# Two weight sums formed on the Vector engine instead of by adding DMAs, in a fused two-layer block on one Trainium2 core

## The chip, the cores and the metric

The program runs on 1 core of a Trainium2 chip. A core has a matrix engine (TensorE: PE in the rows, PEld for its weight loads), a Vector engine (DVE), a Scalar engine (ACT), GpSimd (POOL), a Sync engine (SP) whose queue issues most DMAs, and 16 DMA engines that move data between the chip's memory and the on-chip memory. The metric is the device time of one execution in microseconds (us), lower is better. The kernel before takes 2440.25 us (median of 3 runs, 2436.58 to 2447.19).

## The reference

The reference runs one sequence of 256 rows, 2048 wide, through a mixer layer, a pooling layer and an attention layer. All of it is computed in float32. What the change touches is the feed-forward part that follows the mixer and the pooling, twice in all:

```python
for i in range(2):
    ...                                    # mixer (i = 0) or pooling (i = 1), residual into x
    h = rmsnorm(x, g[2])                   # 256 x 2048
    f = jnp.square(jax.nn.relu(h @ mlp_w1[i])) @ mlp_w2[i]   # 2048 -> 8192 -> 2048
    x = x + rmsnorm(f, g[3])
```

## The kernel before

**Split products.** Every float32 weight tile (128 partitions x 2048 numbers, 1 MB) is split on the chip into a high part (ACT, line 495, two halves of 1024) and a low part (DVE, line 614, raw minus high, again two halves). A product is three matrix multiplications: high x high, high x low, low x high (line 351). A tile feeds 12 of them when 128 rows are multiplied and 24 when 256 are. The high and low parts live in a ring of 3 operand buffers, so the split of a tile waits until the tile three places earlier has been used, half by half. Raw tiles land in a ring of 3 raw buffers (`raw`, loads of line 1015 on SP's queue); a raw buffer is free when its low part is made.

**Up-projection with seven products.** The 8192 columns of `mlp_w1` are worked off in 8 blocks of 1024 columns. The first block is a plain product. For each of the 7 other blocks (`both_ways`, e = 1 to 7), which I call a round, rows, depth and columns are each halved and the 2x2 block product is formed with seven instead of eight products, Winograd's way. With B11, B12 (left half of the depth, two column halves of 512) and B21, B22 (right half), the seven steps use these weights, each of two tiles (j = 0, 1):

- up 1: B11. up 2: B21. up 3: B22.
- up 5: B11+B12, called T1. up 6: B11+B12+B22. up 4: B11+B12+B22+B21.
- up 7: B12+B22, called T3.

B11, T1 and the two longer sums are one chain: two fixed buffers in `R_f` (`chain`) are loaded with B11 by SP (`chain_load`, line 1019), and after each split of them `link` lets a DMA from POOL's queue add the next block to them in place (`chain_add`, line 1007). T3 is made in the raw ring: SP loads B12 and a POOL DMA adds B22 to it (`add_tile`, line 1002). POOL's engine only issues these DMAs.

**Order of a round.** Down-projection tiles of the block before (`down`, 24 multiplications, two banks that are freed by DVE's `R_m` sums of line 599) stand between the up steps, which take turns in two other banks. The tiles of a round in order, with up steps of two tiles and down steps of one: up 1, down 0, up 2, down 1, up 5, down 2, up 3, down 3, up 6, down 4, up 7, down 5, up 4, down 6, four pairs of transposes (line 354), down 7. The outputs of the seven products are put together from staging tiles `EV` by DVE (`combine`, line 599) and squared by ACT (lines 551 and 553: relu, square). What each engine does is written in one fixed order: `take` and `release` emit the splits of tiles some places ahead, and each engine works its own list strictly in order. So a split that stands behind a `combine` in DVE's list waits for it, and a relu that stands before a split in ACT's list holds it up.

**Around it.** `x_columns` normalizes and transposes the residual `X` (2 MB, resident all the time) ahead of a projection; for a projection with no filler work between, it splits the first weight tile in four quarters. At the start of the program tiles 0 to 2 of `w_z` land at once and tile 3 waits for a raw buffer.

## Time and profile before

| | before |
|---|---|
| median of 3 runs | 2440.25 us |
| the profiled execution | 2433.57 us |
| its span | 2431.7 us |
| PE busy | 95% |
| DVE busy | 67% |
| ACT busy | 54% |
| POOL busy | 5% |
| granted TensorE clock, mean | 0.978 |
| DMA | 563.60 MB, mean 232 GB/s |

PE's share is high, but the end of a multiplication is modelled in the records, so "busy" isn't the same as full pace. The profiled execution is 6.7 us below the median of the runs; steps are worked out against the former and then set beside the latter. The rounds of the two feed-forward parts lie between about 454 and 1112 us and between about 1283 and 1940 us of the span.

### The profile page before, as it was taken

The page shows a single profiled execution, that of the slowest core. Times are in us where ns is not written, and L with a number is a line of the kernel's source. Part 1 is how long each engine was busy: PE and PEld are TensorE (multiplying, and loading weights), DVE is VectorE, ACT ScalarE, POOL GpSimd, SP SyncE. Part 2 cuts the span into 40 slices and gives each one's busy share as a digit, 9 for nine tenths or more (in the row PEclk, how much of TensorE's full clock was granted, in tenths as well). Part 3 has the DMA queues.
Part 4 walks back from the last instruction along what each step waited for, and adds up shares of the span by engine and source line. Part 5 has one row for each costly group of instructions (what it writes and reads, how often), then busy time and mean ns, then how long its engine had stood idle before and what let it go on. Part 6 is the DMA issues. An engine that isn't in the chain of part 4 may idle for free.

```text
span 2431.7 us, 26613 instructions
## 1 busy us (share of the span) xinstructions
PE 2312.5 (95%) x10609; PEld 1898.8 (78%) x10609; DVE 1623.3 (67%) x2015; ACT 1321.8 (54%) x1769; POOL 127.4 (5%) x160
## 2 busy tenths in 40 slices
PE   9999999999889899899999989899899899999998
PEld 6778888778778677777887777787777788888887
DVE  5665856866667667667877667667666676556764
ACT  6355445655646556555666646556556555444453
POOL 0000000001001001010001000000000001000000
PEclk9999999999999999999999999999999999999999
DMA  8444545889899898896658898998998845653343
GB/s 332 157 173 173 184 164 190 239 279 275 277 278 254 262 294 254 257 283 228 225 208 233 272 289 252 262 293 264 254 283 269 251 141 201 244 214 129 140 172 121
DMA packets 80299, 563.60 MB, mean 232 GB/s; under 512 B 9033, under 2 KB 9364, under 8 KB 14319
## 3 DMA queue, kind: packets, MB, share of 16 engines
q1 hardware_dynamic: 61568, 429.58, 47.1%
q0 software_dynamic: 18464, 132.20, 26.2%
q8 instruction: 84, 1.38, 0.2%
q14 instruction: 39, 0.32, 0.0%
q10 hardware_dynamic: 144, 0.12, 0.0%
HBM read 559.77 MB, written 2.10 MB: 231 GB/s over the span
## 4 chain that ended last, share of the span: by engine, by line
PE 59%; DMA 23%; DVE 9%; ACT 4%; issue 2%; POOL 1%; ACTq 0%; POOLq 0%; DVEq 0%
PE P L351 56%; DMA R_f<-in_w_u 15%; DVE low L614 7%; DMA raw<-in_w_d 5%; ACT hi L495 3%; DMA raw<-in_w_u 3%; PE P L354 3%; DVE EV L599 1%; DVE R_m L599 1%; ACT EV L551 1%; POOL raw L1002 0%; ACT R_h L490 0%; POOL R_f L1007 0%; DVE R_f_r L599 0%; DVE X L602 0%
## 5 line engine op out<-in xcount | busy, mean ns | idle before, releaser
L614 DVE TENSOR_TENSOR low<-raw,hi 128x1024 fp32r<-128x1024 f32 (+3 forms) x752 | 879.6, 1203 | 535.8 <-ACT hi L495 532.7
L495 ACT ACTIVATE hi<-raw 128x1024 fp32r<-128x1024 f32 (+3 forms) x752 | 758.3, 1039 | 551.2 <-PE P L351 315.4
L351 PE MATMUL P<-hi,R_h 128*128 128x512 f32 (+2 forms) x2944 | 954.9, 395 | 8.4 <-DVE low L614 8.1
L351 PE MATMUL P<-hi,R_f_r 128*128 128x512 f32 x2480 | 822.4, 405 | 96.7 <-DVE R_m L599 52.7
L351 PEld LDWEIGHTS P<-hi,R_h 128*128 128x128 f32 x2944 | 554.4, 189 | 131.4 <-DVE low L614 12.7
L351 PEld LDWEIGHTS P<-hi,R_f_r 128*128 128x128 f32 x2480 | 483.7, 195 | 211.9 <-DVE low L614 109.1
L351 PE MATMUL P<-low,R_h 128*128 128x512 f32 (+2 forms) x1472 | 572.4, 389 | 0.0
L351 PE MATMUL P<-low,R_f_r 128*128 128x512 f32 x1240 | 497.6, 401 | 0.0
L614 DVE TENSOR_TENSOR low<-R_f,hi 128x1024 fp32r<-128x1024 f32 x224 | 264.5, 1221 | 94.1 <-ACT hi L495 92.4
L351 PEld LDWEIGHTS P<-low,R_h 128*128 128x128 f32 x1472 | 278.0, 189 | 56.3 <-issue 4.3
L495 ACT ACTIVATE hi<-R_f 128x1024 fp32r<-128x1024 f32 x224 | 227.7, 1052 | 100.6 <-DMA R_f<-in_w_u 66.4
L351 PEld LDWEIGHTS P<-low,R_f_r 128*128 128x128 f32 x1240 | 242.6, 196 | 49.4
L351 PE MATMUL P<-hi,R_g_r 128*128 128x512 f32 x448 | 142.6, 389 | 0.0
L551 ACT ACTIVATE EV<-EV,st 128x512 f32<-128x512 f32 x56 | 40.5, 723 | 167.5 <-DVE EV L599 167.5
L1007 POOL DMA_DIRECT2D R_f<-in_w_u x84 | 78.0, 1039 | 871.7 <-DVE low L614 871.7
L351 PEld LDWEIGHTS P<-hi,R_g_r 128*128 128x128 f32 x448 | 84.1, 188 | 17.4
L351 PE MATMUL P<-low,R_g_r 128*128 128x512 f32 x224 | 87.2, 389 | 0.0
L599 DVE TENSOR_TENSOR R_m<-P,R_m 128x512 f32<-128x512 f32 x112 | 71.9, 683 | 0.0
L351 PE MATMUL P<-hi,R_s_r 128*128 128x512 f32 x224 | 71.3, 389 | 0.0
L354 PE MATMUL P<-ident,EV 128*128 128x128 f32 (+1 forms) x476 | 66.4, 272 | 0.0
L354 PEld LDWEIGHTS P<-ident,EV 128*128 128x128 f32 (+1 forms) x476 | 56.7, 139 | 9.1
L599 DVE TENSOR_TENSOR R_f_r<-P,R_f_r 128x512 fp32r<-128x512 f32 x66 | 42.6, 684 | 26.4 <-ACT R_f_r L490 26.4
(216 smaller groups left out, 1260.4 us busy)
## 6 DMA issues: line engine op xcount, KB each, us to landing
raw<-in_w_d SPq DMA_DIRECT2D x128, 1024.0 KB, 8.4
raw<-in_w_u SPq DMA_DIRECT2D x100, 1024.0 KB, 5.2
R_f<-in_w_u POOLq DMA_DIRECT2D x84, 1024.0 KB, 11.9
raw<-in_w_z SPq DMA_DIRECT2D x46, 1024.0 KB, 4.9
raw<-in_w_i SPq DMA_DIRECT2D x36, 1024.0 KB, 4.8
R_f<-in_w_u SPq DMA_DIRECT2D x28, 1024.0 KB, 7.9
raw<-in_w_u POOLq DMA_DIRECT2D x28, 1024.0 KB, 10.4
raw<-in_w_mo SPq DMA_DIRECT2D x16, 1024.0 KB, 4.9
```

What stands on the lines that cost most here:

```text
L351: return self.e.matmul(o, l, r, start=start, stop=stop, skip_group_check=True)
L354: return self.e.transpose(o, i, self.m.ident[0:i.shape[0], 0:i.shape[0]])
L495: self.e.activation(hi, raw, ACT.Copy).then_inc(*self.inc("high_made", ("high", k, d)))
L551: self.e.activation(o, p, ACT.Relu, scale=r).then_inc(*self.inc("act_done", evacuated))
L599: self.e.tensor_tensor(o, a, b, op).then_inc(*self.inc("dve_done", *done))
L614: self.e.tensor_tensor(low, raw, hi.bitcast(f32), ALU.subtract).then_inc(*self.inc("low_made", *lows))
L1007: self.e.dma_start(o, i, accum_op=ALU.add).then_inc(*self.landed(f"added{j}", done))
```

## The change

1. T1 and T3 are formed by DVE. Two more fixed buffers, `chain[2]` and `chain[3]`, hold B12; they are the memory of `X`. Once B11 has been split, DVE adds B12 onto it (`first_sum`, giving T1 in `chain[j]`). B22 is loaded once, as a plain raw tile of kind "kept"; after its split DVE adds it onto B12 (`third_sum`, giving T3 in `chain[j + 2]`), and only then its raw buffer is free. `add_tile` is gone, and `link` keeps two adding DMAs per j, for B22 and B21.
2. `X` is stored to a scratch tensor in the chip's memory after the first up group (`keep_x`), and is loaded again after the last round (`back`), before the residual needs it.
3. Products 1 and 2 accumulate in one bank, and products 5 and 3 in the other. Copies of products 1 and 5 are taken in between, and the multiplications of the second product wait for that copy (`onto`). DVE's `combine` of products 1+2 and of 5+3 goes; the bank of 5+3 is read by the second `combine` after up 6 and is free after it.
4. Tile 3 of `w_z` gets its own landing place in `R_f` and isn't behind the raw ring.
5. In `x_columns` the last sums of row half 0 (`out_of`, `squares_of`) stand ahead of the first two quarter splits.

```diff
@@ -149,6 +149,7 @@
 NO = 3
 AHEAD = 2
 CHAIN = (0, 4, 6, 2)
+FIRST = 3
...
-        self.chain = [R_f[:, 4096:6144], R_f[:, 6144:8192]]
+        self.chain = [R_f[:, 4096:6144], R_f[:, 6144:8192], self.X[:, 0, :], self.X[:, 1, :]]
+        self.first_raw = R_f[:, 0:2048]
...
+    def tile_sum(self, o, i, ready, done):
+        self.wait_ge(ready)
+        self.tt(o, o, i, ALU.add, done)
...
-    def load_tile(self, k, o, i, l, free):
-        self.wait_ge(free)
-        self.e.dma_start(o, i).then_inc(*self.landed(f"ring{l % NL}", ("loaded", k)))
+    def load_tile(self, k, o, i, ring, free):
+        self.wait_ge(free)
+        self.e.dma_start(o, i).then_inc(*self.landed(ring, ("loaded", k)))
...
-                raw = m.raw[l % NL][0:parts, 0:c]
-                E.load_tile(k, raw, a[name][i], l, freed.get(l - NL))
-                if kind == "sum":
-                    E.add_tile(k, raw, a[name][more], l)
+                E.load_tile(k, m.raw[l % NL][0:parts, 0:c], a[name][i], f"ring{l % NL}", freed.get(l - NL))
+            elif k == FIRST:
+                E.load_tile(k, m.first_raw, a[name][i], "ring3", None)
...
         if kind == "chain":
-            raw, ready = m.chain[more[3]], ("chained", *more)
+            raw, ready = m.chain[more[3] + 2 * (more[2] == 4)], ("chained", *more)
+        elif k == FIRST:
+            raw, ready = m.first_raw, ("loaded", k)
         else:
-            raw, ready = m.raw[l % NL], ("tile sum", k) if kind == "sum" else ("loaded", k, 2 * d // n) if k < 2 else ("loaded", k)
+            raw, ready = m.raw[l % NL], ("loaded", k, 2 * d // n) if k < 2 else ("loaded", k)
...
                 link(*more, ("low", k, 3))
-            else:
+            elif kind == "load" and l is not None:
                 freed[l] = ("low", k, 3)
                 load_ahead()
...
     def link(mlp_, e, s, j, free):
-        s, e = (s + 1) % 4, e + (s == 3)
-        i, done = 8 * e + CHAIN[s] + j, ("chained", mlp_, e, s, j)
-        if e == 8:
-            chain_last[j] = free
-        elif s == 0:
-            E.chain_load(j, m.chain[j], a[f"w_u{mlp_}"][i], free, done)
+        w = a[f"w_u{mlp_}"]
+        if s == 0:
+            return
+        if s in (1, 2):
+            E.chain_add(j, m.chain[j], w[8 * e + CHAIN[s + 1] + j], free, ("chained", mlp_, e, s + 1, j))
+        elif e == 7:
+            chain_last[j + 2 * (s == 4)] = free
+        elif s == 3:
+            E.chain_load(j, m.chain[j], w[8 * e + 8 + j], free, ("chained", mlp_, e + 1, 0, j))
         else:
-            E.chain_add(j, m.chain[j], a[f"w_u{mlp_}"][i], free, done)
-
-    chain_last = [None, None]
+            E.chain_load(j + 2, m.chain[j + 2], w[8 * e + 12 + j], free, ("linked", mlp_, e + 1, j))
+
+    chain_last = [None] * 4
...
         if filler is None:
             quarter = quarters()
+            out_of(0)
+            squares_of(0)
             quarter(0)
             quarter(1)
-            out_of(0)
-            squares_of(0)
             start(0, lambda: (quarter(2), quarter(3)))
...
+
+        def keep_x():
+            kept = side_load("kept", a["x_kept"], m.X.rearrange("p t n -> p (t n)"), list(x_m))
+            for j in range(2):
+                E.chain_load(j + 2, m.chain[j + 2], a[up_w][12 + j], [kept, list(h_m), list(r_m)], ("linked", l, 1, j))
...
                 if g == 0:
+                    keep_x()
...
-        def half_product(b, xh, xl, ready, tiles, end, soon):
+        def half_product(b, xh, xl, ready, tiles, end, soon, onto, aside):
 
             for n, tile in enumerate(tiles):
                 j, wh, wl = take(up_w, *tile)
+                if n == 0:
+                    aside()
                 wh, wl = v3(wh, 4), v3(wl, 4)
                 for k in range(4):
-                    x = ready[4 * n + k] if isinstance(ready, list) else ready
+                    x = [ready[4 * n + k] if isinstance(ready, list) else ready, onto]
                     whose = ([("product", j, 1)] if k == 3 else []) + ([("used", j, k // 2)] if k % 2 else [])
                     E.product(P[b][:, :], xh[:, 4 * n + k, :], xl[:, 4 * n + k, :], wh[:, k, :], wl[:, k, :], j, k,
-                              n == k == 0, n == 1 and k == 3, x, bank_free[b], *whose)
+                              onto is None and n == k == 0, n == 1 and k == 3, x, bank_free[b], *whose)
                 if n == 1 and soon:
                     end(b, ("product", j, 1))
                 release(j, ("product", j, 1))
...
+            def copied(n, b, done):
+                k, name = ev(hold=True), mark("product copied")
+                E.copy_out(EV[k][:, :], P[b][:, :], done, ev_free[k], name)
+                ks[n], ms[n] = k, name
+
             def first(b, done):
-                k, name = ev(hold=True), mark("product 1")
-                E.copy_out(EV[k][:, :], P[b][:, :], done, ev_free[k], name)
-                bank_free[b] = [name]
-                ks[1], ms[1] = k, name
+                copied(1, b, done)
 
             def second(b, done):
-                k = ev(hold=True)
-                c11 = combine(k, P[b][:, :], EV[ks[1]][:, :], ALU.add, [done, ms[1]], ev_free[k])
-                bank_free[b] = [c11]
-                ks[11] = k
-                ms[11] = relu_square(k, EV[k][:, :], 0, c11, None)[1]
-                ms[1] = c11
+                ks[11] = k = ev(hold=True)
+                evacuated, ms[11] = relu_square(k, P[b][:, :], 0, done, ev_free[k])
+                bank_free[b] = [evacuated]
 
             def fifth(b, done):
-                k, name = ev(hold=True), mark("product 5")
-                E.copy_out(EV[k][:, :], P[b][:, :], done, ev_free[k], name)
-                bank_free[b] = [name]
-                ks[5], ms[5] = k, name
+                copied(5, b, done)
 
             def third(b, done):
-                k = ev(hold=True)
-                ks[12] = k
-                ms[12] = combine(k, P[b][:, :], EV[ks[5]][:, :], ALU.add, [done, ms[5]], ev_free[k])
-                bank_free[b] = [ms[12]]
+                box["w"] = b, done
 
...
             def sixth(b, done):
                 ms[1] = combine(ks[1], P[b][:, :], EV[ks[1]][:, :], ALU.add, [done, ms[1]])
                 bank_free[b] = [ms[1]]
-                c12 = combine(ks[12], EV[ks[12]][:, :], EV[ks[1]][:, :], ALU.subtract, [ms[12], ms[1]])
-                ms[12] = relu_square(ks[12], EV[ks[12]][:, :], 0, c12, None)[1]
-                ms[1] = c12
+                wb, w_done = box["w"]
+                ks[12] = k = ev(hold=True)
+                c12 = combine(k, P[wb][:, :], EV[ks[1]][:, :], ALU.subtract, [w_done, ms[1]], ev_free[k])
+                bank_free[wb] = [c12]
+                ms[12] = relu_square(k, EV[k][:, :], 0, c12, None)[1]
...
             def seventh(b, done):
                 ms[1] = combine(ks[1], P[b][:, :], EV[ks[1]][:, :], ALU.add, [done, ms[1]])
                 bank_free[b] = [ms[1]]
                 c22 = combine(ks[5], EV[ks[5]][:, :], EV[ks[1]][:, :], ALU.subtract, [ms[5], ms[1]])
                 ms[5] = relu_square(ks[5], EV[ks[5]][:, :], 1, c22, None)[1]
-                ms[1] = c22
...
+            kept_at = at_["take"] + 9
+
+            def first_sum(j):
+                E.tile_sum(m.chain[j], m.chain[j + 2], [("chained", l, e, 0, j), ("linked", l, e, j)], ("chained", l, e, 1, j))
+
+            def third_sum(j):
+                k = kept_at + j
+                landed = None if listing else plan[k][6]
+                done = ("chained", l, e, 4, j)
+                E.tile_sum(m.chain[j + 2], m.raw[(landed or 0) % NL][:, :], [("linked", l, e, j), ("loaded", k)], done)
+                if not listing:
+                    freed[landed] = done
+                    load_ahead()
...
             up(1, 0, HH[:, HLEFT, TOP], HL[:, HLEFT, TOP], h_left, linked(0), first)
-            down(0)
-            up(2, 1, HH[:, HRIGHT, TOP], HL[:, HRIGHT, TOP], h_right, plain(b21), second)
+            down(0, lambda: first_sum(0))
+            up(2, 0, HH[:, HRIGHT, TOP], HL[:, HRIGHT, TOP], h_right, plain(b21), second, onto=ms[1], aside=lambda: first_sum(1))
             if e == 1:
                 flush()
             down(1)
-            up(5, 0, SH[1], SL[1], s_m[1], linked(1), fifth)
-            down(2)
-            up(3, 1, SH[4], SL[4], s_m[4], plain(b22), third)
+            up(5, 1, SH[1], SL[1], s_m[1], linked(1), fifth)
+            down(2, lambda: third_sum(0))
+            up(3, 1, SH[4], SL[4], s_m[4], plain(b22, "kept"), third, onto=ms[5])
             down(3)
-            up(6, 0, SH[2], SL[2], s_m[2], linked(2), sixth)
+            up(6, 0, SH[2], SL[2], s_m[2], linked(2), sixth, aside=lambda: third_sum(1))
             down(4)
-            up(7, 1, SH[3], SL[3], s_m[3], added, seventh)
+            up(7, 1, SH[3], SL[3], s_m[3], linked(4), seventh)
             down(5)
             up(4, 0, HH[:, HRIGHT, BOTTOM], HL[:, HRIGHT, BOTTOM], h_right, linked(3), fourth, True)
...
         row_m.append(side_load("gain", m.gain_row, a["rows"][row].partition_broadcast(128), chain_last[0]))
+        back = [side_load(f"back{t}", m.X[:, t, :], a["x_kept"][:, 2048 * t:2048 * t + 2048], chain_last[2 + t]) for t in range(2)]
```

How the lists move. First DVE's list before, in a round, from the splits of the tiles of up 3 and down 3 to those of up 4 (`low<-raw` is the split of a raw tile, `low<-R_f` that of a chain tile, `R_m` the sum of a down bank, `EV` a combine; x6 stands for six in a row, two per tile):

```order
L614 TENSOR_TENSOR low<-raw,hi 128x1024 [waits s_high_made] x6
L614 TENSOR_TENSOR low<-R_f,hi 128x1024 [waits s_high_made] x4
L599 TENSOR_TENSOR EV<-P,EV 128x512 [waits s_act_done,s_product_done]
L614 TENSOR_TENSOR low<-raw,hi 128x1024 [waits s_high_made] x2
L599 TENSOR_TENSOR R_m<-P,R_m 128x512 [waits s_product_done]
L599 TENSOR_TENSOR R_m<-P,R_m 128x512
L614 TENSOR_TENSOR low<-raw,hi 128x1024 [waits s_high_made] x4
L599 TENSOR_TENSOR EV<-P,EV 128x512 [waits s_dve_done,s_product_done]
L599 TENSOR_TENSOR EV<-EV 128x512 [waits s_dve_done]
L614 TENSOR_TENSOR low<-raw,hi 128x1024 [waits s_high_made] x2
L614 TENSOR_TENSOR low<-R_f,hi 128x1024 [waits s_high_made] x4
L599 TENSOR_TENSOR EV<-P,EV 128x512 [waits s_dve_done,s_product_done]
```

The same place of DVE's list in the changed kernel:

```order
L616 TENSOR_TENSOR low<-raw,hi 128x1024 [waits s_high_made] x4
L601 TENSOR_TENSOR X<-X,raw 128x2048 [waits s_ring1]
L616 TENSOR_TENSOR low<-raw,hi 128x1024 [waits s_high_made] x2
L616 TENSOR_TENSOR low<-R_f,hi 128x1024 [waits s_high_made] x4
L616 TENSOR_TENSOR low<-raw,hi 128x1024 [waits s_high_made] x2
L601 TENSOR_TENSOR R_m<-P,R_m 128x512 [waits s_product_done]
L601 TENSOR_TENSOR R_m<-P,R_m 128x512
L601 TENSOR_TENSOR X<-X,raw 128x2048 [waits s_ring2]
L616 TENSOR_TENSOR low<-X,hi 128x1024 [waits s_high_made] x4
L601 TENSOR_TENSOR EV<-P,EV 128x512 [waits s_act_done,s_product_done]
L601 TENSOR_TENSOR EV<-P,EV 128x512 [waits s_dve_done]
L616 TENSOR_TENSOR low<-raw,hi 128x1024 [waits s_high_made] x2
```

The combine after up 3 is gone, a tile sum stands behind the splits of up 3's tiles and another one behind the sums of down 3, and up 7's tiles are split from `X` behind it. Both combines after up 6 now read a bank, and they stand behind up 7's splits.

SP's list in one round before (`in_w_d` are down tiles, `in_w_u` up tiles, `R_f` the chain):

```order
L1015 DMA raw<-in_w_u 128x2048 [waits s_low_made] x2
L1015 DMA raw<-in_w_d 128x2048 [waits s_low_made] x2
L1015 DMA raw<-in_w_u 128x2048 [waits s_low_made] x2
L1015 DMA raw<-in_w_d 128x2048 [waits s_low_made] x2
L1015 DMA raw<-in_w_u 128x2048 [waits s_low_made] x2
L1015 DMA raw<-in_w_d 128x2048 [waits s_low_made] x4
L1019 DMA R_f<-in_w_u 128x2048 [waits s_low_made] x2
```

And in the changed kernel, from the same chain loads on:

```order
L1016 DMA raw<-in_w_u 128x2048 [waits s_low_made] x2
L1016 DMA raw<-in_w_d 128x2048 [waits s_low_made] x2
L1016 DMA raw<-in_w_u 128x2048 [waits s_low_made] x2
L1016 DMA raw<-in_w_d 128x2048 [waits s_low_made]
L1016 DMA raw<-in_w_d 128x2048 [waits s_dve_done] x2
L1016 DMA raw<-in_w_d 128x2048 [waits s_low_made] x2
L1020 DMA X<-in_w_u 128x2048 [waits s_low_made] x2
L1016 DMA raw<-in_w_d 128x2048 [waits s_low_made]
L1020 DMA R_f<-in_w_u 128x2048 [waits s_low_made] x2
```

The two later loads of up tiles per round (B12 for T3) are gone, two loads into `X` are new, and two down tiles (those of down 4 and down 5) now wait for DVE's tile sums instead of a split. The load of down 6 stands behind them.

## Rows read from the trace of the kernel before

**Rows 1.** the page, part 1, whole span: busy time, share of the span, instructions.

```profile
PE 2312.5 (95%) x10609; PEld 1898.8 (78%) x10609; DVE 1623.3 (67%) x2015; ACT 1321.8 (54%) x1769; POOL 127.4 (5%) x160
```

**Rows 2.** windows, four rounds: length, busy us (instructions) by engine, PEclk, DMA, GB/s.

```profile
737.80:833.20 95.40, 87.14 (x378) 70.83 (x377) 63.41 (x63) 52.79 (x59) 6.98 (x8) 0.96 0.91 265
...
sum 378.70, PE 349.72 PEld 285.19 DVE 254.16 ACT 213.24 POOL 28.18; mean PE 87.43 PEld 71.30 DVE 63.54 ACT 53.31 POOL 7.05
```

**Rows 3.** the chain of waits, 735 to 930 us: start us, us, what.

```profile
737.81 19.10 PE P L351 x84
...
776.87 5.20 DMA raw<-in_w_u
...
783.42 26.69 DMA R_f<-in_w_u
...
814.23 0.70 DVE EV L599
...
817.32 2.36 DVE low L614 x2
819.68 0.61 DVE R_m L599
...
820.42 8.27 PE P L351 x24
828.70 0.87 PE P L354 x8
```

**Rows 4.** timeline of PE, 797 to 836 us: start, us, what [idle before, releaser].

```profile
803.81 0.50 PE L351 MATMUL P<-hi,R_f_r 128*128 128x512 f32 x1 [3.14 <-DVE low L614]
...
820.42 0.76 PE L351 MATMUL P<-hi,R_f_r 128*128 128x512 f32 x1 [4.89 <-DVE R_m L599]
```

**Rows 5.** timeline of PE, 533 to 545 us.

```profile
536.36 0.47 PE L351 MATMUL P<-hi,R_f_r 128*128 128x512 f32 x1 [2.25 <-ACT R_m L490]
...
536.90 0.62 PE L351 MATMUL P<-hi,R_f_r 128*128 128x512 f32 x2
```

**Rows 6.** DMA, 642.2 to 1020.8 us: queues; issues, KB, median us to landing.

```profile
q0 software_dynamic: 4769, 34.74, 45.9%
q1 hardware_dynamic: 9216, 67.11, 45.6%
...
raw<-in_w_d SPq DMA_DIRECT2D x32, 1024.0 KB, 8.8
```

**Rows 7.** source line 599, 0 to 460 us: duration ns min/median/max, starts.

```profile
L599 DVE TENSOR_TENSOR R_f<-R_f x2: 2291/2292/2294, 114.8 to 117.1; 128x2048 f32<-128x2048 f32 x2
```

**Rows 8.** timeline of ACT, 800 to 803 us.

```profile
800.17 0.72 ACT L551 ACTIVATE EV<-EV,st 128x512 f32<-128x512 f32 x1 [2.88 <-DVE EV L599]
800.93 0.63 ACT L553 ACTIVATE EV<-EV 128x512 f32<-128x512 f32 x1
801.46 1.99 ACT L495 ACTIVATE hi<-raw 128x1024 fp32r<-128x1024 f32 x2
```

**Rows 9.** waits of PE, whole span: us in total, times, longest.

```profile
PE P L351 <- DVE R_m L599: 52.7, 12, 4.9
PE P L351 <- DVE low L614: 47.4, 28, 3.1
```

**Rows 10.** DMA issues, whole span: KB each, median us to landing.

```profile
R_s<-in_memt POOLq DMA_DIRECT2D x1, 2048.0 KB, 12.8
```

**Rows 11.** timeline of PE, 0 to 30 us.

```profile
26.00 0.47 PE L351 MATMUL P<-hi,R_h 128*128 128x512 f32 x1 [1.89 <-DVE low L614]
```

**Rows 12.** timeline of all engines, 1980 to 1992 us.

```profile
1984.19 1.05 DVE L614 TENSOR_TENSOR low<-raw,hi 128x396 fp32r<-128x396 f32 x2 [3.25 <-ACT hi L495]
...
1985.16 0.68 DVE L599 TENSOR_TENSOR R_m<-P,R_m 128x512 f32<-128x512 f32 x1
...
1988.67 1.42 DVE L602 SCALAR_TENSOR_TENSOR X<-R_m,st,X 128x512 f32<-128x512 f32 x2
1989.48 1.78 PE L354 MATMUL P<-ident,X 128*128 128x128 f32 x8 [3.24 <-DVE X L602]
```

More of the change, by code:

```diff
@@ L343 @@
         product = norm_mean = norm_part = norm_whole = norm_root = relu_square = residual = rope = rope_keys = scale = scaled_parts = scores = side_load = side_taps = sine = sine_of = \
[L344 removed]
+        split = square_sum = store = tile_sum = chain_load = chain_add = combine = operand_sum = times_row = times_row_apart = pads = group_sums = tail_keys = tail_rows = turn = v_times_k = values = warm = y_back = idle
 class Pe(Engine):
@@ L997, in side_load @@
         self.e.dma_start(o, i).then_inc(*self.landed(sem, done))
-    def add_tile(self, k, o, i, l):
-        self.wait_ge(("loaded", k))
-        self.e.dma_start(o, i, accum_op=ALU.add).then_inc(*self.landed(f"sum{l % NL}", ("tile sum", k)))
     def chain_add(self, j, o, i, free, done):
@@ L1137, in take @@
             l = o = None
-            if kind != "chain":
+            if kind != "chain" and j != FIRST:
                 l = numbers["landing"]
@@ L2017, in mlp @@
         flush()
-        return residual(sums, gm, gain_apart if late else gain_of, out_of, squares_of, apart=late)
+        return residual(sums, gm, gain_apart if late else gain_of, out_of, squares_of, back, late)
     memory = {}
```

17 lines of the change are left out of this document (8 added, 9 removed).

## The prediction

> **What bounds the kernel now.** I read the page first: PE is busy for 95% of the span, DVE for 67% [rows 1]. That says where to look for losses: not in an engine that is full, but in the places where PE stands. PE's own waits give two large groups, 52.7 us behind DVE's sums of the down banks and 47.4 us behind low parts [rows 9]. Nearly all of both lie in the 14 rounds.
>
> Next, the windows over four whole rounds: 378.7 us, so 94.7 us a round, with the DMA engines 0.91 busy and DVE at 63.5 us a round [rows 2]. What would a round take if PE never stood? 84 multiplications at full pace took 19.10 us, 0.2274 us each [rows 3]. A round has 7 up steps and 8 down steps of 24, so 360 multiplications: 81.9 us. Two groups of transposes at 0.87 us [rows 3] bring it to 83.6 us. So about 11.1 us a round are lost, 155 us in 14 rounds.
>
> The chain of waits says to what. In the round from 737.8 us it leaves PE, goes to the landing of a raw up tile (5.20 us), then to one adding DMA that took 26.69 us, then through a combine (0.70), a split (2.36) and a bank's sum (0.61) back to PE [rows 3]. PE's timeline shows the two holes: 3.14 us before down 5 and 4.89 us before down 6 [rows 4]. After the second the first multiplication takes 0.76 us instead of 0.50 [rows 4], and the 24 of down 6 take 8.27 us [rows 3] instead of 24 x 0.2274 = 5.46. So a round loses about 8.0 us by standing and 2.8 us by half pace.
>
> Why is the adding DMA that slow? In 378.6 us the adding queue q0 moved 34.74 MB, which is 33 tiles, and held the 16 engines for 45.9%: 5.27 us a tile. The plain queue q1 moved 64 tiles in 45.6%: 2.70 us a tile [rows 6]. A round has 8 adds and 16 plain loads, 42.2 + 43.2 = 85.4 us of 94.7. The DMA engines are nearly full, and everything that is late is late behind them.
>
> **The change part by part.**
>
> DMA: a round now has 4 adds and 16 plain loads (the chain's B11, X's B12, B21, B22, eight down tiles): 21.1 + 43.2 = 64.3 us. In a round of 85 us that is 0.75. Before, the two adds for T3 and the chain's last two are issued close together, and the landing of 26.69 us is one of these; the adds that remain are two pairs, three steps apart.
>
> DVE: four tile sums of 128x2048 are added. A DVE sum of that shape took 2.29 us [rows 7], so +9.2 us. Two combines go, -1.4 us. DVE comes to 63.5 + 7.8 = 71.3 us a round. ACT's work stays: its copies are the same, and the relu of products 1+2 reads the bank. PE still has 360 multiplications, and the copies of products 1 and 5 that it now waits for lie beside down 0 and down 2, 5.46 us each.
>
> Where does DVE's list end last? I set up 1 at 0 and count PE in steps of 5.46: down 3 ends at 43.7, up 6 at 49.1, down 4 at 54.6. The first tile sum stands before down 1's split; from the round before's list DVE gets there at about 10.5, and up 5's tiles are ready at 20.0 and 22.4, wanted at 21.8 and 24.5. The tile sum for j=0 of T3 ends at 33.6; down 4's load waits for it and has until 42 to land, 8.4 us.
> The tight place begins at 43.7, when down 3 has freed its operand. High half 1.05, low half 1.2, two bank sums of 0.65: 47.2. Tile sum: 49.5. Splits of up 7's two tiles: 54.2. Two combines of 0.7: 55.6. Up 7 wants at 54.6 the bank that the second combine frees, so PE stands 1.0 us. Then ACT's relu and square, 1.3 us [rows 8], high half 1.0, low 2.4: down 5's tile is ready from 59.1, wanted at 61.1. Its load was free to start at 49.5 (it waits for the tile sum) and is wanted at 56.9, so 7.4 us; down tiles landed in 8.8 us (median) in the crowded stretch [rows 6]. At 0.75 instead of 0.91 I take it as just in time. Splits of up 4: 65.0, combines 66.4, ACT 67.7, split of down 6 to 71.2, bank sum 71.8, wanted at 72.0. So by this timetable 1.0 us is lost, at the start of up 7. Several margins are under 1 us, so I take 2.0 us: a round of 85.6 us.
>
> Does half pace come back with a hole that short? After a hole of 2.25 us the next multiplications ran at full pace, two in 0.62 us [rows 5]; the hole of 4.89 us [rows 4] was followed by half pace. I take none. The Trainium skill speaks against me: TensorE: Matmul & The Clock Gate, section "A second HAM failure mode: psum-queue depth-cycling", has small idle times between groups of matmuls, repeated, that let the clock go back and forth. Rows 5 do not agree with it for one such hole; no row shows holes of 1 us in each round.
>
> The rounds: 94.7 - 85.6 = 9.1 us, x 14 = 127 us.
>
> X's store and reload: 2 MB out, beside the second up group. The nearest row is a 2 MB load on the same queue, 12.8 us [rows 10]. SP's two loads into X wait for it with the loads of later tiles behind them. Counted from the start of the second up group, the store lands at 12.8, the two X tiles by about 22 (8.8 for the first), the next raw tile, up 2's second, at 25. It is wanted after four tiles of that group, up 1, down 0 and half of up 2, 35.5, less its split, so at 33. Cost 0. If the store took twice as long, the first round would stand 5 us, twice in the program: bounds 0 and +10 us. The reload starts with the last splits of up 7 and has down 5 to down 7 and eight more down tiles, over 50 us: 0.
>
> Tile 3's own place: PE stood 1.89 us for it at 26.00 us [rows 11]. Its load now doesn't wait for a split, but the columns of the input are still being prepared on ACT and DVE: -1.5 us, bounds 0 and -3.
>
> The order at the tail: row half 0's last bank sum of DVE ran at 1985.16, behind a quarter's splits of 1984.19 that wait for PE, and X followed at 1988.67 with PE standing 3.24 us [rows 12]. The bank had been finished one group of multiplications earlier. Ahead of the splits, the sum and the root can be done before PE is through: -3 us here, -1 us ahead of the first feed-forward part, bounds 0 and -5.
>
> Sum against the profiled execution: 2433.6 - 127 - 1.5 - 4 = 2301. The median of the runs is 6.7 us above the profiled execution, so 2308; for the margins under 1 us, which can only fail on one side, I add a fifth of a microsecond a round and say 2311.
>
> **The rivals.**
>
> *DVE takes over (A).* DVE has 71.3 us of work in 85.6, and after each combine it waits for ACT's relu, square and high half, 2.4 us, three times a round: 78.5 us. If a raw tile is late by 2 us at down 4 or down 5, or a split slips, the loss before up 7 and down 6 grows to what it is now less the clock's part, 5 to 6 us a round. For it: the chain already runs through combines and splits [rows 3]. Against: today the same list starts late only because it waits for DMAs. Round 89.1: 5.6 x 14 = 78, time 2440 - 78 - 5 = 2357.
>
> *Half pace stays (B).* The holes shrink but the clock still drops once a round: 2.8 x 14 = 39 us more, 2350. It is the mechanism of the skill's page above, priced by rows 3.
>
> *The raw ring chokes (C), the other side.* Two of three raw buffers are held by B22 until DVE's tile sums, and SP's list stops there with the loads of down 4, 5, 6 and 7, and behind them X's and the chain's. If landing from that point took 20 us or more, as the add of 26.69 us did [rows 3], down 5 would be 12.6 us late each round, more than the 11.1 that can be won: 14 x 1.5 = 21 us slower and up, 2460. It decides from a landing of about 18.5 us. Against: plain loads took 8.8 us (median) even at 0.91 [rows 6].
>
> *The transfers were hidden anyway (D).* If down 5 and 6 were held by the combines' place in the list alone, nothing changes: 2435. Against: DVE sat waiting for landed tiles in just these holes.
>
> **How the numbers follow.** Forecast 0.68, A 0.17, B 0.08, C 0.03, D 0.04. Range: PE's floor gives 2440 - 155 + a little for pauses that can't go, so 2290 at the low end; the high end takes in B and A, 2362. A measurement of this kernel can tell about 0.5%, 12 us, from no change. Faster by more: 0.93 (forecast, A, B). Within: 0.04 (D). Slower: 0.03 (C).
>
> **What would show it.** Rounds of 85 to 86 us in the windows, DMA share near 0.75, DVE near 71 us a round. PE's holes of 3.1 and 4.9 us gone, a new one of about 1 us at the first multiplication of up 7, PEclk at 1.0 in the rounds. The 128x2048 sums at 2.29 us. No wait of SP's list over 15 us behind `kept`. No hole at 26.0 us and a shorter one before the attention projection. I am wrong if down 4 or down 5 waits for its landing in most rounds, or if the hole before down 6 is still over 3 us.

## The result and the profile after

| | before | after |
|---|---|---|
| median (runs) | 2438.41 us (4) | 2308.36 us (4) |
| lowest to highest | 2434.93 to 2447.19 | 2307.69 to 2310.81 |
| ratio [95%] | | 0.946 [0.944, 0.949] |
| the profiled execution | 2433.57 us | 2310.81 us |
| its span | 2431.7 us | 2309.0 us |
| granted TensorE clock, mean | 0.978 | 0.996 |

The change makes the kernel 5.4% faster. The forecast was 2311 us. The page's part 1 of the kernel after (busy us, share of the span, instructions) answers to [rows 1]:

```profile
PE 2272.0 (98%) x10609; PEld 1873.5 (81%) x10609; DVE 1717.7 (74%) x2043; ACT 1318.4 (57%) x1769; POOL 81.1 (4%) x110
```

The windows of the kernel after over eleven whole rounds, each from one up 7 to the next (one of the eleven rows, and their sum; columns as in [rows 2]):

```profile
771.50:856.50 85.00, 84.01 (x376) 69.01 (x376) 70.56 (x70) 54.16 (x67) 4.25 (x5) 1.00 0.74 242
...
sum 935.80, PE 922.66 PEld 760.09 DVE 768.29 ACT 581.00 POOL 39.48; mean PE 83.88 PEld 69.10 DVE 69.84 ACT 52.82 POOL 3.59
```

935.8 / 11 = 85.07 us a round against 94.7 [rows 2]. The granted clock is 1.00 in all eleven, and the DMA engines are busy for 0.74 to 0.78 of a round instead of 0.91. The holes of 3.14 and 4.89 us [rows 4] are gone. PE's three largest waits in the whole span (total us, times, longest), beside [rows 9]:

```profile
PE P L353 <- DVE EV L601: 10.7, 12, 0.9
PE P L353 <- DVE low L616: 9.2, 5, 2.9
PE P L353 <- DVE R_m L601: 3.5, 5, 1.1
```

52.7 us behind the bank sums became 3.5, and 47.4 behind low parts became 9.2. New is the first row: one hole of 0.9 us in 12 of the 14 rounds, behind a `combine`. PE's timeline of the kernel after shows where (start, us, what, [idle before, releaser]); R_h starts up 7:

```profile
482.61 0.80 PE L353 MATMUL P<-hi,R_s_r 128*128 128x512 f32 x1 [2.91 <-DVE low L616]
483.63 1.06 PE L353 MATMUL P<-hi,R_s_r 128*128 128x512 f32 x2
...
489.48 0.61 PE L353 MATMUL P<-hi,R_f_r 128*128 128x512 f32 x2
...
856.53 0.47 PE L353 MATMUL P<-hi,R_h 128*128 128x512 f32 x1 [0.89 <-DVE EV L601]
...
874.19 0.47 PE L353 MATMUL P<-hi,R_f_r 128*128 128x512 f32 x1 [1.06 <-DVE R_m L601]
...
1866.16 1.32 PE L356 MATMUL P<-ident,X 128*128 128x128 f32 x8 [1.59 <-DVE X L604]
```

The first rows are the first round of a part: a hole of 2.91 us, then two multiplications in 1.06 us instead of 0.61 for about 6 us; the granted clock from 483.61 to 489.61 us was 0.57, near the lower of its two levels, 1.2 GHz. The last row is the tail: 1.59 us instead of 3.24 [rows 12].

The path into the 0.9 us hole is DVE's. Its timeline of the kernel after, from the place where down 3 frees its operand (844.78 us; ACT's high half starts there, and the second of the first two low halves waits for it):

```profile
844.57 2.56 DVE L616 TENSOR_TENSOR low<-raw,hi 128x1024 fp32r<-128x1024 f32 x2
847.04 1.28 DVE L601 TENSOR_TENSOR R_m<-P,R_m 128x512 f32<-128x512 f32 x2
848.24 2.28 DVE L601 TENSOR_TENSOR X<-X,raw 128x2048 f32<-128x2048 f32 x1
850.44 4.62 DVE L616 TENSOR_TENSOR low<-X,hi 128x1024 fp32r<-128x1024 f32 x4
854.98 1.41 DVE L601 TENSOR_TENSOR EV<-P,EV 128x512 f32<-128x512 f32 x2
```

Low parts, bank sums, T3's second tile sum, up 7's splits, two combines: 844.78 to 856.39 us, and PE starts up 7 at 856.53. Nothing in it waits for a transfer. The DMA view of the kernel after, 620 to 970 us (packets, MB, share; issues with KB and median us to landing):

```profile
q1 hardware_dynamic: 9444, 68.72, 49.8%
q0 software_dynamic: 2448, 17.83, 25.9%
...
raw<-in_w_d SPq DMA_DIRECT2D x32, 1024.0 KB, 8.8
...
R_f<-in_w_u POOLq DMA_DIRECT2D x16, 1024.0 KB, 10.2
...
R_s<-in_mem POOLq DMA_DIRECT2D x1, 1024.0 KB, 5.6
```

68.72 MB are 65.5 tiles and 0.498 x 350 us is 174.3: 2.66 us a plain tile. The 17 tiles of q0 held the 16 engines for 90.7 us, 5.33 us each. One of them, `R_s<-in_mem`, is a plain load; at 2.66 us it leaves 88.0 us for 16 adds, 5.50 each. The 33 tiles of [rows 6] hold the same plain load, which the prediction counted as an add: 5.35 instead of 5.27 for the 32 adds. The prices are nearly those of before; there are only half as many adds.

### The profile page after: what moved, and what is told of

Read it like the earlier page. It is cut to its first block, busy times and chain, and to the rows that moved or that the text cites. A ratio compares the mean times of both kernels' runs of the same rounds, so it can differ in the third digit from the quotient of the medians.

```text
span 2309.0 us, 26586 instructions
## 1 busy us (share of the span) xinstructions
PE 2272.0 (98%) x10609; PEld 1873.5 (81%) x10609; DVE 1717.7 (74%) x2043; ACT 1318.4 (57%) x1769; POOL 81.1 (4%) x110
## 4 chain that ended last, share of the span: by engine, by line
PE 82%; DVE 10%; DMA 3%; ACT 2%; issue 1%; POOL 0%; ACTq 0%; POOLq 0%; DVEq 0%
PE P L353 80%; DVE low L616 6%; DMA raw<-in_w_d 3%; PE P L356 3%; ACT hi L497 1%; DVE R_m L601 1%; DVE X L601 1%; DVE EV L601 1%; DVE R_f L601 0%; DVE R_f_r L601 0%; DVE X L604 0%; ACT EV L553 0%; DVE R_h L604 0%; DVE R_g_r L601 0%; DVE st L604 0%
## 5 line engine op out<-in xcount | busy, mean ns | idle before, releaser
L616 DVE TENSOR_TENSOR low<-raw,hi 128x1024 fp32r<-128x1024 f32 (+3 forms) x694 | 810.2, 1200 | 409.1 <-ACT hi L497 406.5
L497 ACT ACTIVATE hi<-raw 128x1024 fp32r<-128x1024 f32 (+3 forms) x694 | 701.7, 1040 | 473.9 <-PE P L353 332.4
L353 PE MATMUL P<-hi,R_f_r 128*128 128x512 f32 x2480 | 792.8, 392 | 5.3 <-DVE R_m L601 3.5
L353 PEld LDWEIGHTS P<-hi,R_f_r 128*128 128x128 f32 x2480 | 465.8, 188 | 107.4 <-DVE low L616 7.7
L353 PE MATMUL P<-low,R_f_r 128*128 128x512 f32 x1240 | 482.9, 389 | 0.0
L353 PEld LDWEIGHTS P<-low,R_f_r 128*128 128x128 f32 x1240 | 233.1, 188 | 46.5
L553 ACT ACTIVATE EV<-EV,st 128x512 f32<-128x512 f32 x42 | 30.4, 724 | 152.8 <-DVE EV L601 152.8
L1008 POOL DMA_DIRECT2D R_f<-in_w_u x56 | 48.7, 869 | 1027.2 <-DVE low L616 1027.2
L497 ACT ACTIVATE hi<-X 128x1024 fp32r<-128x1024 f32 x56 | 57.6, 1057 | 32.0 <-DVE X L601 24.9
L616 DVE TENSOR_TENSOR low<-X,hi 128x1024 fp32r<-128x1024 f32 x56 | 64.7, 1218 | 0.0
## 6 DMA issues: line engine op xcount, KB each, us to landing
X<-in_w_u SPq DMA_DIRECT2D x28, 1024.0 KB, 12.8
```

The costliest lines, as they stand in the source:

```text
L353: return self.e.matmul(o, l, r, start=start, stop=stop, skip_group_check=True)
L497: self.e.activation(hi, raw, ACT.Copy).then_inc(*self.inc("high_made", ("high", k, d)))
L553: self.e.activation(o, p, ACT.Relu, scale=r).then_inc(*self.inc("act_done", evacuated))
L616: self.e.tensor_tensor(low, raw, hi.bitcast(f32), ALU.subtract).then_inc(*self.inc("low_made", *lows))
L1008: self.e.dma_start(o, i, accum_op=ALU.add).then_inc(*self.landed(f"added{j}", done))
```

## The experiments

Each was run beside the kernel before on the same chip. Its median was 2434.4 us beside e1 to e4, 2438.3 beside e5 to e8, 2440.1 beside e9 to e11 and 2438.3 beside e12, so ratios are what compare, and a difference of two ratios is uncertain by 0.003 to 0.004. "b" is a diff against the kernel before, "a" against the kernel after.

| run | median us | ratio [95%] |
|---|---|---|
| kernel after | 2308.4 | 0.946 [0.944, 0.949] |
| e1: before, adds as plain loads | 2290.2 | 0.941 [0.939, 0.943] |
| e2: before, product pairs | 2425.2 | 0.996 [0.995, 0.998] |
| e3: after, no product pairs | 2312.7 | 0.950 [0.948, 0.952] |
| e4: T3 by DVE, T1 by DMA | 2293.1 | 0.942 [0.940, 0.944] |
| e5: T1 by DVE, T3 by DMA | 2473.1 | 1.014 [1.011, 1.018] |
| e6: after, 4 more adds a round | 2396.3 | 0.983 [0.980, 0.987] |
| e7: after, banks swapped | 2307.2 | 0.947 [0.944, 0.949] |
| e8: after, edges undone | 2310.8 | 0.948 [0.945, 0.951] |
| e9: e4 + e7 | 2292.2 | 0.939 [0.938, 0.941] |
| e10: e4, no product pairs | 2300.8 | 0.943 [0.941, 0.944] |
| e11: e9 + rows early | 2290.1 | 0.938 [0.937, 0.940] |
| e12: e11, banks as in e4, sum ahead | 2287.2 | 0.938 [0.936, 0.941] |

### Is it the adding?

**e1_plain_adds** (b): the same transfers at the same places, issued as plain copies. The sums themselves are left out: only the last block lands.

```diff
-        self.e.dma_start(o, i, accum_op=ALU.add).then_inc(*self.landed(f"sum{l % NL}", ("tile sum", k)))
+        self.e.dma_start(o, i).then_inc(*self.landed(f"sum{l % NL}", ("tile sum", k)))
...
-        self.e.dma_start(o, i, accum_op=ALU.add).then_inc(*self.landed(f"added{j}", done))
+        self.e.dma_start(o, i).then_inc(*self.landed(f"added{j}", done))
```

> The kernel before, with its 8 adding DMAs a round issued as plain loads from the same queue at the same places (the weight sums are left out of the result: only the last block lands). Lists of all engines are those of before. Theory T (the DMA engines are nearly full with the adds, so tiles land late, and that makes the holes): 24 plain loads x 2.70 us = 64.8 us a round instead of 85.4, DMA share about 0.7, holes before down 5 and down 6 go, rounds 85 to 86 us, time about 2310 to 2320. Rival R (the combines' places in the lists make the holes, whatever the DMA engines do): rounds stay at 94 us, time 2430 to 2440.

Measured: 2290.2 us. Windows and DMA of e1, 620 to 970 us:

```profile
620.00:970.00 350.00, 350.00 (x1585) 290.61 (x1585) 268.28 (x272) 229.50 (x262) 19.24 (x36) 1.00 0.80 301
```

```profile
q1 hardware_dynamic: 9423, 68.55, 52.6%
q0 software_dynamic: 5040, 36.70, 27.5%
```

PE is busy for all 350 us, which is why the time lies 20 us below the expected one: nothing is left of the waits in these rounds. q0's 35 tiles cost 0.275 x 350 / 35 = 2.75 us each instead of 5.27, and no tile is late. So the loss of the kernel before is the price of adding, not the number of bytes and not the order of the lists: e1 moves more GB/s (301) than the kernel before (265 in [rows 2]) and never stands.

**e6_traffic** (a): the reverse. Four adding DMAs a round of 1 MB, from memory to a scratch tensor that nobody reads.

```diff
+    def idle_add(self, i, free):
+        self.wait_ge(free)
+        n = self.counts.value.get("idle", 0) // 16
+        self.e.dma_start(self.a["x_idle"][n], i, accum_op=ALU.add, max_dma_last_dim=8192).then_inc(*self.landed("idle"))
```

> The changed kernel with 4 more adding DMAs of 1 MB a round on the adding queue, from w_u into scratch in the chip's memory that nobody reads, two where the add for T1 was issued before and two just before T3's tile sums. No engine but the queue waits for them. The destination is memory, not the on-chip tile, so their time may differ from 5.27 us. Theory T: DMA share back over 0.9, chain adds and down tiles late, holes of several us a round, 2350 to 2440. Theory T2: the chain's last adds are late behind the extra ones but T3 isn't: 2310 to 2350. Rival R: 2308.

Measured: 2396.3 us. Waits of PE in the whole span and windows, 620 to 970 us, of e6:

```profile
PE P L353 <- DVE low L616: 66.9, 31, 3.5
```

```profile
620.00:970.00 350.00, 329.95 (x1465) 269.45 (x1464) 274.62 (x260) 206.89 (x243) 28.77 (x34) 1.00 0.93 278
```

As many adds as before bring back two thirds of what had been won (88 of 130 us), but not the waits of the kernel before. The chain of waits of e6, before down 5:

```profile
693.85 2.21 DVE X L601
696.08 11.78 DMA raw<-in_w_d
```

Its split follows, and PE starts down 5 at 710.25, 2.50 us late. What is late is a plain down tile: its load starts when DVE's tile sum has freed the raw buffer, and down tiles took 11.8 us (median) instead of 8.8. That is rival C's link at a lower price. The chain's adds landed in 10.5 us (median), as in the kernel after. So e6 shows that adding traffic in the background costs the rounds time; it does not show the link through which the kernel before lost it. That is left to e4 and e5.

### Which sum pays?

**e4_t3_by_dve** (a): T1 by adding DMAs again, T3 stays with DVE.

```diff
-        if s == 0:
-            return
-        if s in (1, 2):
+        if s in (0, 1, 2):
...
-            down(0, lambda: first_sum(0))
+            down(0)
```

> The changed kernel with T1 formed by an adding DMA of B12 again and T3 still by DVE: 6 adds and 16 plain loads a round, 31.6 + 43.2 = 74.8 us of DMA. Theory T in its simple form (share of the DMA engines alone counts): share 0.87, partway back, 2330 to 2370. Theory T2 (only the burst of T3's two adds beside the chain's last two is late): no loss, and DVE has 4.6 us a round less: 2300 to 2310. Rival R: as the changed kernel, 2308.

**e5_t1_by_dve** (a): the other half. `first_sum` stays, T3 is made in the raw ring by `add_tile` again.

```diff
+            if kind == "sum":
+                E.add_tile(k, m.raw[l % NL][:, :], a[name][more], l)
...
-            down(2, lambda: third_sum(0))
+            down(2)
...
-            up(7, 1, SH[3], SL[3], s_m[3], linked(4), seventh)
+            up(7, 1, SH[3], SL[3], s_m[3], [(8 * e + 4 + j, "sum", b22[j]) for j in range(2)], seventh)
```

> The mirror of the last one: T1 formed by DVE, T3 by a load into the raw ring and an adding DMA as before. 6 adds and 18 plain loads a round, 31.6 + 48.6 = 80.2 us of DMA. Theory T2 (the add into the raw ring for T3, issued close to the chain's last two adds and waited for by up 7's splits, is what is late; T1's add isn't): holes before down 5 and down 6 stay, 2400 to 2440. Theory T (share of the DMA engines alone): 0.9, so about as far back as T3 by DVE alone was with 0.89: about 2295 to 2330.

Measured: e4 2293.1 us, e5 2473.1 us. One half of the change is worth more than the whole, the other half alone is slower than the kernel before. Windows (620 to 970 us) and waits of PE, first of e4, then of e5:

```profile
620.00:970.00 350.00, 346.42 (x1560) 286.06 (x1559) 273.95 (x269) 221.73 (x259) 22.98 (x27) 1.00 0.89 274
```

```profile
PE P L353 <- DVE EV L601: 10.6, 12, 0.9
PE P L353 <- DVE low L616: 4.3, 2, 3.2
```

```profile
620.00:970.00 350.00, 315.10 (x1380) 257.65 (x1379) 244.44 (x239) 197.05 (x232) 18.77 (x22) 0.95 0.82 259
```

```profile
PE P L353 <- DVE EV L601: 112.9, 14, 10.5
PE P L353 <- DVE R_m L601: 17.8, 12, 2.4
```

The DMA share doesn't order them: e4 is at 0.89 and has only the 0.9 us hole, e5 is at 0.82 and stands 5.9 to 10.5 us before each up 7. Part of e5's low share is that its rounds are longer, but the work of the DMA engines per round doesn't order the kernels either: about 85 us in the kernel before, 80 in e5, 75 in e4.

What PE waits for before up 7 in e5 is T3's own second add. POOL issues it at 696.89 us, after waiting for the load of B12 under it. The timelines of ACT and DVE of e5, with up 7 starting at 714.06:

```profile
709.13 2.00 ACT L497 ACTIVATE hi<-raw 128x1024 fp32r<-128x1024 f32 x2 [4.91 <-DMA raw<-in_w_u]
710.22 2.36 DVE L616 TENSOR_TENSOR low<-raw,hi 128x1024 fp32r<-128x1024 f32 x2 [4.56 <-ACT hi L497]
712.50 1.41 DVE L601 TENSOR_TENSOR EV<-P,EV 128x512 f32<-128x512 f32 x2
```

The add has landed after 12 us, its split follows, and behind it in the list the two combines that free up 7's bank. The chain of waits of e5 names the transfer behind the next hole, before down 6:

```profile
697.97 25.98 DMA R_f<-in_w_u
...
725.06 2.36 DVE low L616 x2
727.42 0.61 DVE EV L601
```

It is the same link as in [rows 3] (26.69 us there): the chain's last add, issued behind the two adds of T3. The kernel before has both: T3's second add ahead of the hole before down 5, the chain's last ahead of the one before down 6. With T3's adds gone no chain add took over 14.1 us (e4, 500 to 1100 us; 27.1 in the kernel before), though T1's two are there. So what costs is T3's two adds, not four adds more in a round; T1's are issued right after up 1's splits and had room. How much of it is the bundle of four, and how much the order of POOL's list, is not separated: the chain's last two adds stand there behind the wait for B12's landing too, and e4 takes away both. Nor was it taken further why e5 is over 40 us slower than e2, the kernel before with the pairs alone, and above its expected range; in its chain of waits the two plain loads ahead of the adds took 11.5 and 6.8 us instead of the 8.7 and 5.2 of the kernel before.

And why does e4 beat the kernel after, by 11 us in the ratios and 15 in the medians? Both have the same 0.9 us hole. Set the starts of up 7 in the two profiled executions against each other. From the marker ahead of the rounds to up 7 of the second round the kernel after takes 195.1 us and e4 190.1; from the last up 7 of the first part to up 7 of the second part's second round 340.2 and 334.2. So the opening of each part costs 5 to 6 us. Another 0.85 us on average goes in each of the five rounds between in the first part, in holes before down 6 (behind `R_m`) that e4 doesn't have: 15.2 us together. The chain of waits of the kernel after, first round, shows DVE's list from end to end:

```profile
464.14 2.35 DVE low L616 x2
466.50 1.20 DVE R_f_r L601 x2
467.69 0.18 DVE R_f L601
...
472.16 1.14 DVE R_g_r L601
473.30 2.20 DVE R_f L601
...
481.43 1.15 DVE low L616
```

In this round DVE also makes the sums of the operands (`R_f_r`, `R_g_r`), and the T1 tile sums (`R_f`, 467.69 and 473.30) come on top. The list ends 2.91 us late, and half pace follows here; the hole of 2.90 us at the same place of the second part (1251.54) is followed by full pace. e4 has no hole of that kind there; one of 1.04 us comes at 515.16 us, at full pace.

### The product pairs

**e2_pairs_only** (b) and **e3_no_pairs** (a): item 3 of the change alone, and the change without it. Both are the same edit, one way and the other:

```diff
-                E.copy_out(EV[k][:, :], P[b][:, :], done, ev_free[k], name)
-                bank_free[b] = [name]
...
-                c11 = combine(k, P[b][:, :], EV[ks[1]][:, :], ALU.add, [done, ms[1]], ev_free[k])
+                evacuated, ms[11] = relu_square(k, P[b][:, :], 0, done, ev_free[k])
```

> The kernel before plus only the accumulation of products 1+2 and 5+3 in one bank each; the sums stay adding DMAs. Theory T: late landings stay, 2425 to 2445 (two combines of 0.7 us a round less on DVE, none of them on the late chain; at most 1 us a round, 14 us). Rival R: the two combines gone from DVE's list take most of the holes away, 2330 to 2370.

> The changed kernel with the products combined by DVE as before, sums still by DVE. Theory T: DVE gets 1.4 us a round more, 71.2; the bank of up 7 is free earlier, so the hole of 0.9 us before it goes; the splits behind the combines come later by up to 1.4 us. 2305 to 2320. Rival R: the holes come back, 2380 or more.

Measured: e2 2425.2, e3 2312.7 us. The pairs are worth 9 us on the kernel before. On top of the sums they are worth 9 us by the ratios (0.950 against 0.946) and 4 by the medians, which come from different chips; the intervals of the ratios touch. PE's waits in e2 tell of a side effect:

```profile
PE P L351 <- DVE EV L599: 81.4, 14, 8.0
PE P L351 <- DVE R_m L599: 19.7, 12, 2.9
```

The bank of 5+3 is free only after up 6's second combine, and in e2 that stands in DVE's list behind splits of a T3 tile that lands late: PE stands before up 7 (7.47 us at 517.09) instead of before down 5, and for less before down 6 (19.7 us in all against 52.7). The landing was the cause in both places.

**e10_t3_no_pairs** (a) is e4 with e3's edit.

> T3 by DVE, T1 by an adding DMA, products combined by DVE as before (no accumulation in one bank). The hole of 0.89 us before up 7 goes, as the bank isn't held; DVE has 1.4 us a round more. If DVE isn't the bound here: 12 x 0.89 = 11 us faster than T3 by DVE alone, 2282. If the 2 combines delay the splits behind them: 2293 or more.

Measured: 2300.8 us, beside 2292.2 of e9 on the same chip, which differs from it by the pairs and by two swapped banks (worth nothing in e7, below). That is 8 us, as much as the ratios give in the two cases above, and the second case of what was expected. PE's timelines show where most of it lies: e10 has a hole of 2.71 and one of 2.74 us in the opening rounds of the two parts (485.17 and 1246.94), followed by a granted clock of 0.72 and 0.76 for 6 us, and e9 has none there.

### The hole that is left

**e7_banks** (a): up 7 uses the other bank, which is free long before, and up 4 the one of 5+3.

```diff
-            up(7, 1, SH[3], SL[3], s_m[3], linked(4), seventh)
+            up(7, 0, SH[3], SL[3], s_m[3], linked(4), seventh)
...
-            up(4, 0, HH[:, HRIGHT, BOTTOM], HL[:, HRIGHT, BOTTOM], h_right, linked(3), fourth, True)
+            up(4, 1, HH[:, HRIGHT, BOTTOM], HL[:, HRIGHT, BOTTOM], h_right, linked(3), fourth, True)
```

> The changed kernel with the banks of up 7 and up 4 swapped, so that up 7 takes the bank that the first combine after up 6 frees, not the one of the second. If the hole of 0.89 us before up 7 is the wait for that bank, it shrinks by one combine, 0.69 us, to 0.2: at most 12 x 0.69 = 8 us faster than the changed kernel, 2300; as far as the hole before down 6 then grows instead (DVE's list ends no earlier), less, down to 0.

Measured: 2307.2 us, the same. The hole before up 7 shrinks from 0.89 to 0.16 us, and the holes before down 6 grow from 3.5 us in 5 rounds to 6.7 us in 12, up to 1.3 us each (0.84 at 700.28 us in e7). DVE's list from down 3 to down 6 is as long as before, and PE meets its end at the next place. **e9_t3_banks**, the same on e4, likewise:

> T3 by DVE, T1 by an adding DMA, and the banks of up 7 and up 4 swapped. With the sum of T1 off DVE its list has 4.6 us a round to spare, so the shortened hole before up 7 should not come back before down 6: 12 x 0.72 = 8.6 us faster than T3 by DVE alone (2293), 2284. If DVE's list still ends last, 2292.

Measured: 2292.2 us; ratio 0.939 against 0.942 of e4, intervals that meet.

**e12_sum_ahead** (a; e11 with the banks as in e4) takes work out of that stretch: T3's second tile sum is done inside down 3.

```diff
-            down(3)
-            up(6, 0, SH[2], SL[2], s_m[2], linked(2), sixth, aside=lambda: third_sum(1))
+            down(3, lambda: third_sum(1))
+            up(6, 0, SH[2], SL[2], s_m[2], linked(2), sixth)
```

> T3 by DVE, T1 by an adding DMA, X's rows early, banks of up 7 and up 4 as in the changed kernel, and DVE's second tile sum moved from behind the sums of down 3 to ahead of the split of down 4 (in the middle of down 3). If the chain of a round is the one of the timetable (down 3's operand free, split, bank sums, tile sum, two splits, two combines, ACT, split, bank sum, down 6), 2.3 us of it go ahead of its start: the hole of 0.89 us before up 7 goes and none comes before down 6. 2280. If the holes have another cause, 2290.

Measured: 2287.2 us, the lowest median of all, but with the ratio of e11 (0.938, 6.2% below the kernel before): the step can't be told from zero, and the 2280 expected was missed. The hole before up 7 is gone in most rounds; PE's timeline of e12 shows the one before down 6 still there:

```profile
675.19 0.47 PE L353 MATMUL P<-hi,R_h 128*128 128x512 f32 x1 [0.66 <-DVE EV L601]
...
692.83 0.47 PE L353 MATMUL P<-hi,R_f_r 128*128 128x512 f32 x1 [1.07 <-DVE R_m L601]
```

I had read the two holes as one shortage of DVE's list. The second doesn't follow from the first. It may come from the path combine, relu, square, high half, low part behind up 7's end, which a shorter list ahead of up 7 leaves as it is; that wasn't tested.

### The edges

**e8_no_edges** (a): items 4 and 5 undone.

```diff
-FIRST = 3
+FIRST = -1
...
-            out_of(0)
-            squares_of(0)
             quarter(0)
             quarter(1)
+            out_of(0)
+            squares_of(0)
```

> The changed kernel with its two edits outside the rounds undone (tile 3 of w_z again in the raw ring; the quarter splits again ahead of the last sums). By the forecast these two gave 1.5 + 4 = 5.5 us: 2314. By the two traces the start gave 0.5 and the tail 1.7: 2310.5.

Measured: 2310.8 us, 2.5 us above the kernel after (4 by the ratios), with intervals that overlap: it can't be told from zero. In the trace the tail's hole of 3.2 us is back.

**e11_rows_early** (a): e9, and the rows 2 and 3 of X are loaded ahead of the small tables at the start.

```diff
     first_rows(1)
+    first_rows(2)
+    first_rows(3)
```

> As e9, with the last two parts of X's rows loaded right behind the first two at the start, so that they don't stand behind three loads of w_z that wait for splits. The hole of 3.2 us near 39 us waits for their squares; it should go, with the half pace behind it: 3 to 5 us faster than e9, 2280.

Measured: 2290.1 against 2292.2 us of e9 on the same chip; again within the intervals. In the trace the hole near 39 us is gone, as expected (3.43 us in e9, none over 0.5 in e11).

## Why the prediction was right

**The rounds: 85.6 forecast, 85.07 measured.** Most steps behind it held. The DMA share came out at 0.765 (0.75 forecast), DVE at 69.8 us a round (71.3), the 128x2048 sums at 2.28 us (2.29 of [rows 7]), the timetable from the end of down 3's operand to the last combine at 11.6 us (11.9), the hole before up 7 at 0.89 us (1.0; with the margins I took 2.0). The timetable worked because it wrote DVE's whole list down with durations of the trace, and found the wait that would be last once the transfers were early.

**The sum over the rounds: 127 forecast, 121 measured.** From a marker ahead of the rounds (405.40 us before, 404.89 after) to the one ahead of the attention part (1989.48 and 1866.16) 122.8 us were won; 1.65 of them are the shorter hole at the second marker, so 121.2 are the rounds'. The starts of up 7 in PE's timelines divide them (us; part 1 and part 2 are the two feed-forward parts):

| | marker | part 1, first up 7 | last up 7 | part 2, first up 7 | last up 7 | marker |
|---|---|---|---|---|---|---|
| before | 405.40 | 512.62 | 1077.85 | 1342.60 | 1904.04 | 1989.48 |
| after | 404.89 | 515.55 | 1027.45 | 1282.27 | 1791.20 | 1866.16 |

Between the first and the last up 7 of a part lie six whole rounds. They took 93.9 us before, on the mean of all twelve, and 85.07 after: 8.8 us each. The prediction took its 94.7 from four rounds in a row that were slower than the mean. A round's holes before down 5 and down 6 stand behind its up 7, so the last round of each part has them too: behind the last up 7 of part 2 another 8.8 us were won, and from the last up 7 of part 1 to the first of part 2 9.9. Ahead of the first up 7 of part 1 the kernel after is 3.4 us slower: 105.8 + 8.8 + 9.9 - 3.4 = 121.2. So the factor 14 was right, the 9.1 was 8.8, and the timetable left out the opening, where DVE's list has the operand sums as well. There rival A's mechanism, DVE as the bound, is seen. The total, 2311 forecast and 2308 measured, is closer than its terms, and that is luck: between the two profiled executions 132.5 us were forecast and 122.8 won. The rest of the 130 us between the medians comes from the profiled execution before lying 5 us below its median and the one after 2.5 above.

**What was right for a partly wrong reason.** I gave both tile sums the same credit, 8 adds down to 4. e4 and e5 show that T3 by DVE earns everything and T1 by DVE costs 11 to 15 us. My own note was that the adds of T3 and the chain's last two are issued close together; the step "a round now has 4 adds and 16 plain loads", 64.3 us, then priced only the average. With the average, e4 (6 adds, 0.89) should have been in between, and e5 (6 adds) as good as e4.

**The edges: 5.5 us forecast, 2.5 us measured** (e8, within the uncertainty). At the tail 3.24 us became 1.59, so 1.65 of the 3 us that I had put there. At the start the hole of 1.89 us [rows 11] did go, but PE's timeline of the kernel after has

```profile
38.70 0.80 PE L353 MATMUL P<-hi,R_h 128*128 128x512 f32 x1 [2.46 <-DVE low L616]
```

where the kernel before stood 0.78 us: the start is bound by the preparation of the columns (with the last rows of the input loaded earlier, e11, this hole is gone), and 0.5 us was won by 405 us.

**X's store and reload: 0 forecast.** The DMA issues of the kernel after (KB each, median us to landing) and the waits of SP's queue:

```profile
x_kept<-X POOLq DMA_DIRECT2D x2, 2048.0 KB, 8.3
```

```profile
SPq L1020 <- DMA x_kept<-X: 2.8, 1, 2.8
SPq L1016 <- DVE X L601: 334.7, 28, 16.9
```

The store landed in 8.3 us, not 12.8, and held SP up once for 2.8 us. The second row is the mechanism of rival C: SP does wait for the tile sums, up to 16.9 us, but loads free from there landed in 8.8 us, and C asked for 18.5.

**Half pace (rival B).** None in the steady rounds, as forecast: the granted clock is 1.00, the level of 2.4 GHz, in all eleven windows, though a hole of 0.89 us stands in 12 rounds. Among the rounds it did come once where no step had it, in the first round of the first part (482.61 us), for about 6 us. The Trainium skill (TensorE: Matmul & The Clock Gate, "A second HAM failure mode: psum-queue depth-cycling") has repeated small idle times between groups of matmuls let the clock go back and forth; one such hole in 85 us did not do that here. Whether holes closer together would, no run here shows.

## What to carry to other kernels

Price an adding DMA by its own row, here at twice a plain one, and then ask which one is waited for: move the sum whose landing is waited for, and that crowds the next wanted one, to the engine with slack, and leave the others. Check the engine that takes the work in its fullest round, not in the mean one. When a hole at the end of a fixed list has been closed by a freer buffer, expect it at the next place of the same list. Shortening the list ahead of the hole closed it (e12), though without a gain that can be told from zero.

## What the runs showed of the hardware

- An adding DMA of 1 MB into on-chip memory held all 16 DMA engines for 5.4 to 5.5 us (before, after), the same transfer as a plain copy for 2.75 (e1). Two issued together landed in about 10 us each (median 10.2, after); in a bundle of four the last took 26 ([rows 3], e5).
- Within the range from 1.6 to 3.2 us the length of a hole doesn't tell whether half pace follows, and the first multiplication behind it doesn't either. Timelines of PE in the first round of a part in two kernels, each with the window from 1 to 7 us behind the restart (granted clock third from the end), first after, then e5:

```profile
1251.54 0.50 PE L353 MATMUL P<-hi,R_s_r 128*128 128x512 f32 x1 [2.90 <-DVE low L616]
...
1252.54:1258.54 6.00, 5.61 (x25) 4.30 (x24) 6.00 (x7) 5.55 (x7) 0.88 (x1) 1.00 0.99 184
```

```profile
483.67 0.50 PE L353 MATMUL P<-hi,R_s_r 128*128 128x512 f32 x1 [2.91 <-DVE low L616]
...
714.06 0.76 PE L353 MATMUL P<-hi,R_h 128*128 128x512 f32 x1 [8.73 <-DVE EV L601]
...
484.67:490.67 6.00, 6.00 (x21) 4.73 (x20) 6.00 (x7) 5.55 (x7) 0.88 (x1) 0.72 1.00 184
```

  The first multiplication takes 0.50 us behind both holes of 2.9 us, but the clock then stays at 1.00 in one and falls to 0.72 in the other. In the kernel before it was 1.00 behind the 3.14 us of [rows 4] and 0.74 behind 3.10 us at 521.33. In the traces of all kernels here, holes of 1.6 to 3.2 us were followed by 1.00 at some places and by 0.57 to 0.84 at others, and every hole of over 3.3 us by 0.57 to 0.85. What decides below that stays open.
